# Last down projections by token tiles, norms tile by tile, pooling units in a ring of five banks

## The reference

```python
for l in range(DEPTH):                       # DEPTH = 2
    # mixer: layer 0 conv + sliding window; layer 1 pooling + dilated attention
    xp = xp + mixer(rms_norm(xp, norm_mix[l]))
    xp = xp + cross_attn(rms_norm(xp, norm_ca[l]), mk, mv, w_ca_q[l], w_ca_o[l])
    xp = xp + swiglu(rms_norm(xp, norm_ffn[l]), w_ffn_in[l], w_ffn_out[l])
y = rms_norm(xp, norm_final)

def rms_norm(x, g):
    return x * rsqrt(mean(x * x, axis=-1, keepdims=True) + 1e-6) * g
def swiglu(h, w_in, w_out):                  # hidden width 2816
    g, u = split(h @ w_in, 2, axis=-1)
    return (silu(g) * u) @ w_out
# pooling of layer 1, group g of four, windows 2, 4, 8, 16:
#   uc = (h @ w_in)[group];  d = windowed_mean(uc) - uc;  y = (d @ pool_w[g]) * pool_scale
```

## Time and profile before

| | us |
|---|---|
| median of 3 runs | 3047.67 |
| range of the runs | 3040.66 to 3049.91 |
| profiled execution, its own time | 3039.79 |
| its span in the profile | 3038.0 |
| mean granted clock of TensorE in it | 0.983 of full |

### The profile page before, as it was taken

The page is one execution under the profiler, slowest core; times in us unless marked ns, Lnnn a source line. Parts: engine busy times, 40 slices in busy tenths (PEclk is TensorE's granted clock), DMA queues, the critical chain, the costliest instruction groups (busy, mean ns, idle before and its releaser), DMA issues.

```text
span 3038.0 us, 58274 instructions
## 1 busy us (share of the span) xinstructions
PE 2878.4 (95%) x21187; PEld 2733.0 (90%) x21187; DVE 1646.5 (54%) x3338; ACT 795.4 (26%) x1820; POOL 1319.7 (43%) x1135
## 2 busy tenths in 40 slices
PE   7999999998899999999899998999997999999996
PEld 6888999988899999999787777988897999999996
DVE  5555642258655656556733336522378565565657
ACT  4333322132212221222313335212223211222112
POOL 2222343334556666565221102333335666566561
PEclk9999999999999999999999999999998999999998
DMA  3011133311111111111122211234310111111112
GB/s 128 29 34 35 56 118 126 142 66 42 43 42 55 46 51 55 41 55 49 43 80 77 78 70 57 76 131 140 112 42 28 56 55 41 55 41 55 55 41 70
DMA packets 52534, 198.83 MB, mean 65 GB/s; under 512 B 6960, under 2 KB 14000, under 8 KB 49080
## 3 DMA queue, kind: packets, MB, share of 16 engines
q1 hardware_dynamic: 36912, 130.51, 13.5%
q10 hardware_dynamic: 15504, 66.71, 6.0%
HBM read 184.34 MB, written 13.10 MB: 65 GB/s over the span
## 4 chain that ended last, share of the span: by engine, by line
PE 86%; DVE 7%; issue 3%; ACT 2%; POOL 1%; DMA 0%; ACTq 0%; DVEq 0%; SPq 0%; POOLq 0%
PE linear L696 46%; PE ps_scores L981 12%; PE ps_turned L981 8%; PE ps_mixed L981 4%; PE linear L981 4%; PE ps_mixed L836 2%; PE ps_turned L800 1%; PE ps_turned L1141 1%; PE ps_scores L764 1%; PE ps_mixed L1171 1%; PE ps_scores L1117 1%; DVE g_lo L1803 1%; PE linear L764 1%; PE ps_mixed L832 1%; DVE rs L1773 1%
## 5 line engine op out<-in xcount | busy, mean ns | idle before, releaser
L561 POOL TENSOR_TENSOR w_lo<-w_raw,w_hi 128x512 fp32r<-128x512 f32 x492 | 682.7, 1397 | 257.1 <-ACT w_hi L1251 232.0
L557 POOL TENSOR_SCALAR w_hi<-w_raw 128x512 fp32r<-128x512 f32 x324 | 216.3, 681 | 1210.9 <-PE linear L696 1032.5
L696 PE MATMUL linear<-h_hi,w_hi 128*128 128x344 f32 x1200 | 399.5, 333 | 36.7 <-POOL w_lo L561 13.1
L696 PE MATMUL linear<-h_lo,w_hi 128*128 128x344 f32 x1200 | 387.6, 323 | 0.0
L696 PE MATMUL linear<-h_hi,w_lo 128*128 128x344 f32 x1200 | 387.2, 323 | 0.0
L2195 DVE TENSOR_TENSOR x<-linear,x 128x344 f32<-128x344 f32 x528 | 271.7, 515 | 150.0 <-PE linear L696 147.5
L696 PE MATMUL linear<-hid_hi,w_hi 128*128 128x344 f32 x1056 | 339.6, 322 | 6.9 <-issue 6.8
L696 PE MATMUL linear<-hid_hi,w_lo 128*128 128x344 f32 x1056 | 339.8, 322 | 0.0
L696 PE MATMUL linear<-hid_lo,w_hi 128*128 128x344 f32 x1056 | 339.3, 321 | 0.0
L981 PE MATMUL ps_scores<-c,w_hi 128*128 128x258 f32 x1584 | 307.3, 286 | 21.3 <-DVE c L1990 13.3
L696 PEld LDWEIGHTS linear<-h_hi,w_hi 128*128 128x128 f32 x1200 | 229.1, 191 | 55.5 <-issue 45.9
(11 more groups left out here) (314 smaller groups left out, 6359.6 us busy)
## 6 DMA issues: line engine op xcount, KB each, us to landing
w_raw<-in_w SPq DMA_DIRECT2D x246, 512.0 KB, 3.5
kv_slotc<-in_mem_cache_k ACTq DMA_DIRECT2D x8, 2048.0 KB, 8.1
kv_slotc<-in_mem_cache_v ACTq DMA_DIRECT2D x8, 2048.0 KB, 10.1
kv_slot<-in_dil_k ACTq DMA_DIRECT2D x4, 1536.0 KB, 6.6
kv_slot<-in_dil_v ACTq DMA_DIRECT2D x4, 1536.0 KB, 6.4
out_y<-answer ACTq DMA_DIRECT2D x6, 688.0 KB, 3.4
x<-in_x ACTq DMA_DIRECT2D x2, 1376.0 KB, 10.2
out_dil_v_out<-v ACTq DMA_DIRECT2D x4, 516.0 KB, 3.1
```

The source lines that it names most:

```text
L557: pool.tensor_scalar(out, src, 1.0, 0.0, ALU.mult, ALU.add).then_inc(sem["hi_split"], 1)
L561: return pool.tensor_tensor(out, src, hi.bitcast(F32), ALU.subtract).then_inc(sem[event], 1)
L696: mm = pe.matmul(out, w[:, slot, cols], a, start=(k == 0 and j == 0), stop=(k == n - 1 and j == 2))
```

## The change

- In `ffnend0` and `ffnend1` the down projection runs by tiles: for each tile unit 0's four chunks, then unit 1's. The second weight slot is marked as started only in the last tile. The first tile needs two of the four hidden quarters, not all.
- In layer 0, the sums of squares are no longer 24 adds on DVE but three `tensor_reduce` over the eight squares of a tile. In layer 1, POOL adds them, 21 adds of 128x344; PE multiplies them with one column of `ones`, so that the sum of each token stands on a partition; ACT and DVE take root and reciprocal of 128x2 and 88x1 elements; ACT spreads the result on a diagonal; PE multiplies `ones` with it; and DVE makes `answer` straight from that PSUM bank. The output stores keep their place in ACT's order, behind all of this.
- `pool1` uses banks 0, 1, 2, 6, 7 in turn, without `enter`. `pool_map(0)` stands behind the third unit, `pool_map(3)` behind the v unit. The tables of the pooling part are loaded earlier.
- In the first pair, T2, T3 and T4 of kp 3 are made from B12 and a difference held in `hid_val`; three of the four early low parts of kp 2 are made later; the third to fifth product are read out of their banks ahead of the reciprocals they stood behind; the first two gates are scaled after all three roots. ACT casts the first weight block of the next pair behind the first silu, not behind the fourth.

```diff
     if name == "pool1":
-        return three("dve") * 4
+        return [(b, "dve") for b in (0, 1, 2, 6, 7, 0, 1, 2, 6, 7, 0, 1)]
     if name == "att1pre":
-        return three("dve")
+        return [(b, "dve") for b in (2, 6, 7)]
...
+OTHER_RING = {"pool1": (-2, -1, 0, -2, -2), "att1pre": (-4, -3, -2), "att1_0": (-4, -3, -2)}
...
+                def down_by_tiles(ph, p):
+
+                    for t in range(3):
+                        if t < 2:
+                            pe.wait_ge(sem["hid_lo"], at("hid_lo", ph, 0, 2 + 2 * t))
+                        for u in range(2):
+                            if t == 0:
+                                pe.wait_ge(sem["half_split"], at("half_split", ph, 0, u + 1))
+                            for n in range(4):
+                                chunk(ph, 0, p, u, n, t, n == 0 and t == 2 * u,
+                                      at("unit_split", ph, 0, 2 + u + 1) if t == 0 and n == 0 else None)
+                                p += 1
+                            if l == 1 and t and u == 0:
+                                column_sums(t - 1)
+                                if t == 2:
+                                    spread_inverse(0)
+
+                def column_sums(t):
+
+                    pe.wait_ge(sem["added"], at("added", "into_final", 0, (CH - 1) * (t + 1)))
+                    a, b = TILES[t]
+                    for j, o in enumerate(range(a, b, P)):
+                        m = min(P, b - o)
+                        mm = pe.matmul(sum_banks[t][0:m, 384 + j:385 + j], rs[:, o:o + m], ones[:, 0:1], start=True, stop=True)
+                    mm.then_inc(sem["summed"], 1)
...
+                def spread_inverse(t):
+
+                    pe.wait_ge(sem["diagonal"], at("diagonal", "norm_final", 0, t + 1))
+                    for o in range(0, TILE, P):
+                        m = min(P, TILE - o)
+                        mm = pe.matmul(sum_banks[t][:, o:o + m], ones[0:m, :], diagonal[0:m, t, o:o + m], start=True, stop=True)
+                    mm.then_inc(sem["spread_out"], 1)
...
+                down_by_tiles(f"ffnend{l}", pair(f"ffnend{l}", 0, 0, 0))
+                if l == 1:
+                    column_sums(2)
+                    spread_inverse(1)
+                    spread_inverse(2)
...
+            def behind(g, t):
+
+                if (g, t) in ((0, 1), (1, 0), (1, 1)):
+                    sums(g + t - (g == 0), at("added", "into_mix1", 0, g + t + (g > 0)))
+                if (g, t) == (2, 2):
+                    pe.wait_ge(loads["pool1"], 64)
+                    pool_map(0)
+                if (g, t) in ((3, 0), (3, 2)):
+                    pool_map(1 + t // 2)
...
-                if g:
-                    pool_map(g - 1)
+                         after=lambda t: behind(g, t))
+            unit("att1pre", 0, 0, 0, TILES, h_hi, h_lo, slot=first_slot("att1pre"))
             pool_map(3)
-            enter("att1pre")
-
-            pe.wait_ge(sem["pooled_out"], at("pooled_out", "pool1", 0, 12))
-            unit("att1pre", 0, 0, 0, TILES, h_hi, h_lo, slot=first_slot("att1pre"))
...
+                for n in range(1, CH):
+
+                    pool.wait_ge(sem["squared"], at("squared", "into_final", 0, CH * t + n + 1))
+                    if n > 1:
+                        pool.wait_ge(sem["added"], at("added", "into_final", 0, (CH - 1) * t + n - 1))
+                    pool.sem_inc(gate_sem["pool"], 1)
+                    pool.tensor_tensor(rs[:, a:b], sq_all[:, 0, a:b] if n == 1 else rs[:, a:b], sq_all[:, n, a:b], ALU.add
+                                       ).then_inc(sem["added"], 1)
...
-                gates(f"ffnpre{l}", 0, 0)
-                for b in (0, 1):
-                    cast(b, f"ffnpre{l}", 0, 1, 1, 0)
+                gates(f"ffnpre{l}", 0, 0, 1, {1: lambda: cast(0, f"ffnpre{l}", 0, 1, 1, 0), 3: lambda: cast(1, f"ffnpre{l}", 0, 1, 1)})
...
+
+                for t in range(3):
+                    for n in range(CH):
+                        added(t, n)
+                        past_waits()
+                        square_of(t, n)
+                        if t and n == 5:
+                            root_columns(t - 1)
+                        if t and n == 6:
+                            diagonals(t - 1)
+                root_columns(2)
+                diagonals(2)
...
+                b12, difference = hid_val[:, 0, FIRST], hid_val[:, 1, FIRST]
                 value(2, "B11", "B11")
                 value(3, "B11", "B11")
-                value(3, "T2", "B11")
-                low(2, "B11")
-                low(3, "B11")
                 add(3, 4)
                 dve.wait_ge(sem["freed_dve"], at("freed_dve", source, 3, 5))
-                value(3, "T2", "B12", "above")
+                value(3, None, "B12", b12)
+                low(2, "B11")
+                made(27)
+                count[0] += 1
+                dve.tensor_tensor(difference, b12, combination("val", 3, "B11"), ALU.subtract).then_inc(sem["t_made"], 1)
                 made(28)
-                count[0] += 1
-                dve.tensor_tensor(combination("val", 3, "T2"), combination("val", 3, "T2"), combination("above", 3, "T2"),
-                                  ALU.subtract).then_inc(sem["t_made"], 1)
+                low(3, "B11")
                 dve.wait_ge(sem["tile_done"], at("tile_done", source, 3, 6))
-                made(29)
-                count[0] += 1
-                dve.tensor_scalar(combination("val", 3, "T1"), combination("val", 3, "T2"), -1.0, None, ALU.mult
-                                  ).then_inc(sem["t_made"], 1)
...
+                pre = f"ffnpre{l}"
+                read(pre, 0, 0, 2, None, gate[:, 0, FIRST], None, None)
+                gate_read(pre, 0, 0, 3)
                 inverse_root(0)
+                gate_read(pre, 0, 0, 4, scaled=False)
                 inverse_root(1)
-                dve.wait_ge(sem["rsqrted"], at("rsqrted", ph, 0, 2))
-                gate_read(f"ffnpre{l}", 0, 0, 2)
-                gate_read(f"ffnpre{l}", 0, 0, 3)
                 inverse_root(2)
+                dve.wait_ge(sem["rsqrted"], at("rsqrted", ph, 0, 3))
+                for c, half in QUARTERS[:2]:
+                    dve.tensor_tensor(gate[:, c, half], gate[:, c, half], rs[:, half], ALU.mult).then_inc(sem["gate_ready"], 1)
...
+                    if b == 4:
+                        hid_low(ph, 0, 0)
+                    if b == 5:
+                        hid_low(ph, 0, 2)
+                hid_low(ph, 0, 1)
...
+                    done = 0
+                    for k in range(3 * CH):
+                        add_chunk(k)
+                        if k >= 4 and k % 4 < 3:
+                            low(done)
+                            done += 1
+                    for k in range(done, 2 * CH):
+                        low(k)
+                    total_of_tile(0)
+                    for k in range(2 * CH, 3 * CH):
+                        low(k)
+                    total_of_tile(1)
+                    return
+                for k in range(3 * CH):
+                    add_chunk(k)
+                    if k == 2 * CH - 2:
+                        inverse_columns(0)
+                    if k == 3 * CH - 2:
+                        inverse_columns(1)
+                    if k >= 20:
+                        answer_of(0, k - 20)
+                for c in range(4, CH):
+                    answer_of(0, c)
...
+                dve.tensor_reduce(rs[:, a:b], sq_all[:, :, a:b].rearrange("p c n -> p n c"), AX_X, ALU.add).then_inc(sem["added"], 1)
...
+                    if g == 0 and t == 0:
+                        total_of_tile(2)
+                        dve.wait_ge(sem["added"], at("added", "into_mix1", 0, 3))
+                        chained(dve.memset(pool_u[:, 0:POOL_PAD], 0.0))
```

More of the change, by code:

```diff
@@ L1063, in _ @@
             ffn(0)
-            enter("pool1")
             def pool_map(g):
@@ L2198, in ffn @@
                 order = [(half, t, n) for half in range(2) for t in range(3) for n in range(4)]
-                for b in range(4, 7):
+                for b in (5, 6):
                     gate_read(f"ffnpre{l}", 0, 0, b)
```

283 lines of the change are left out of this document (158 added, 125 removed).

## The result

The changed kernel takes 3013.32 us (median of 4 runs, 3010.11 to 3016.09), the kernel before 3045.94 (median of 4). The ratio is 0.9894, interval 0.9875 to 0.9912: 1.1% faster. The forecast was 2997, range 2984 to 3010. The direction was right, the size was not: the profiled executions differ by 26.5 us in span (3038.0 and 3011.5), where the sum promised 46.5.

A forecast was written before the change was run, and what follows sets the result against it. PE, busy 95%, was taken to bound the kernel, with gains where it waits, mostly for DVE. Terms -28.6, -2.2, -12.4 and -3.3 sum to -46.5, giving 2993.3 from 3039.79, 3001.2 by the median; 2997 was said, range 2984 to 3010.

The forecast's parts named there:

- Pooling stage, the five banks and the maps: Layer 0, down projection's end to v's end: DVE frees banks and means before PE wants them; 64.7 for 93.3, -28.6.
- Pooling stage, the price of the reduction: Layer 0 sums of squares: each reduction of 2752 inputs per partition takes 3.2 us, at 1.18 ns an input.
- slack said to be 2 to 5 us everywhere: Layer 0 pooling stage: DVE has sums, banks and means ready 2 to 5 us early; one us of stalls granted.
- First gate pairs: First gate pair of both layers: DVE's shorter path brings the weight's low part earlier, -6.2 a layer, -12.4 in all.
- four low parts of 0.63: First gate pair, layer 1: DVE's four low parts ahead of the first root priced at 0.63 us each.
- I add 0.8 for contention: First gate pair: 0.8 us allowed for contention, moving the weight's low part from 2321.6 to 2322.4, against 2328.64 before.
- lower bound of 2 a layer: First gate pair: gain of only 2 us a layer if low parts stretch as one of 1.75 did beside POOL.
- Rival A: First gate pair: PE's half-speed products make reads late, keeping 2 to 3 us of 12.4; about 3007, chance 0.14.
- Rival B: Pooling stage: DVE bounds it, POOL stretching its two-input operations; some 9 us come back, 3006, chance 0.12.
- Down projections: Layer 0 down projection: start wait falls from 3.41 to 0.8 us, 2.7 of stalls granted; 26.1 in all, -2.2.
- The end: Layer 1 down projection and output: stores wait in ACT's order, finishing 23.3 us behind PE's last piece; 3034.7 against 3038.0, -3.3.
- Rival E: Pooling stage: strided reduction far dearer, 22 us each removing the whole gain; slower than before, chance 0.02.

The follow-up runs named there:

- experiment 1: Changed kernel with each of the three layer 0 reductions replaced by three additions of halves: 3008.9 us against 3013.3, pooling stage 66.1 us.
- experiment 2: Changed kernel with the third reduction reading neighbouring numbers, not ones 4128 bytes apart (sums then wrong): that reduction 3.02 us in place of 5.28.
- experiment 4: Kernel before, POOL held from weight splits and additions until DVE's last low part: first gate pairs 42.0 and 44.2 us, before 44.9 and 43.1.
- experiment 3: Changed kernel, POOL held until DVE's last low part: splits and additions held, pairs 38.9 and 39.0 us, whole 3010.2; additions alone, 41.3 and 41.4.
- experiment 6: Changed kernel with output stores on SP's queue as answers are made and the third tile's small reciprocal earlier: span ends at 3005.1 us.

## Why the prediction was wrong

- **Pooling stage, the five banks and the maps: right.** No wait for a bank, a window or a mean is left; with the sums in time PE alone fills the stage (66.0 us; 64.7 forecast). The sum's "half of the 0.84 shown for two" misreads its row: those two matmuls are one sum of squares. From start to start the three sums take 1.6 us, so that costs little; the rest of the gap is said in experiment 1.
- **Pooling stage, the price of the reduction: wrong.** The step was "I take the low end, since the row is the same operation, also in a strided order". It measured 1.92 to 2.05 ns an input, not 1.18, 5.3 to 5.6 us a tile. The slack said to be 2 to 5 us everywhere then did not cover two long reductions ahead of the third sum. With the half-speed stretch behind the wait that is 6.7 us (experiments 1 and 2). The bound of 18.3 from the reciprocal was never near, but a value between was there to be taken, and the kernel's own adds of 1.5 ns an element, from SBUF, were the nearer row. The Trainium skill, "VectorE: DVE Perf Modes" (Rules for kernel authors), advised against the reduction; experiment 1 agrees with its advice, experiment 2 shows that for neighbours the operation is no slower than additions.
- **First gate pairs: wrong.** The steps that failed are "four low parts of 0.63" and "I add 0.8 for contention". DVE's operations were counted at the price that they had in layer 1 before, away from POOL's two-input operations. By starting PE's products 3 to 4 us earlier the change let POOL start earlier too, and there the two met; in layer 0, whose timeline the prediction did not read, they had met before (four low parts in 4.00 us, experiment 4) and still do. Held apart, the pair is 3.1 to 3.3 us shorter (experiment 3). Read against 6.2 a layer, the change itself gave 2.9 and 0.8, and 5.9 and 4.1 with POOL held. What layer 1 then lacks is one wait of DVE for the fifth product, 1.16 us, and the factors of the first two roots, 1.27 and 0.98 us beside POOL's held work where the sum had 0.45. The lower bound of 2 a layer named the cause and was still too high for layer 1, which had not paid for it before. (The sum's own terms give 2321.5 and not 2322.4, a slip of 0.9.) The Trainium skill, "SBUF - State Buffer" (Who interferes with whom), says that a DVE operation with two SBUF inputs contends with a POOL operation that reads SBUF; the traces agree (0.63 to 1.71 us). The prediction weighed that rule at the end of the kernel, where nothing came of it, and not here.
- **Rival A had the size, and little of the mechanism.** It kept 2 to 3 us of 12.4; 3.7 were kept. But it blamed PE's products at half speed; with POOL held PE is as slow behind its wait (0.80 for two matmuls) and the gain is there. Half speed does cost something in this pair: the 1.1 us of layer 1 in experiment 4, and perhaps part of the 1.16 above, which was not tried. **Rival B** named POOL stretching DVE's operations, but in the pooling stage, where it cost nothing that experiment 1 did not remove.
- **Down projections: right in kind, in layer 0 half the size in this execution.** The start falls to 0.56 us from 3.41. The stalls are one wait of 1.96 us, and the half-speed stretch behind it, which comes and goes.
- **The end: right.** 23.3 us forecast behind the last piece, 23.2 measured, and the stores did wait for ACT's order (experiment 6). The down projection ahead of it took 28.6 in place of 26.7. POOL's additions took 0.92 each and 0.17 between, 1.09 in place of 0.96, so that PE waited 2.78 us for the last sum.
- **Rival E** did not come: the reduction cost 5.6, not 22.
- **The range was too narrow.** Two terms failed to the same side, and A and B, which have about their sizes, had been taken as exclusive. Both together give 3007 + 9 = 3016, near what came; that is luck in part, since B's 9 us were to come from stretched operations and the 6.7 came from the reductions.

## What to carry to other kernels

Price a strided reduction from a row with its own memory and distance, or add halves: eight squares 4128 bytes apart cost 5.3 us in one reduction and 3.0 in three additions. When the same stage stands in two layers, read both: here layer 0 showed the contention before the change. When a change starts one engine earlier, look up what the engine beside it does in the new interval, and count two-input operations of DVE and POOL that meet at the stretched price. Where several terms share a bias (everything priced quiet), the range must hold them failing together.

## What the runs showed of the hardware

- A TENSOR_REDUCE of 344 outputs from 2752 fp32 inputs in SBUF took 3.02 us with the inputs of a sum next to each other and 5.28 with 4128 bytes between them.
- Two-input fp32 operations of DVE on 516 columns took 0.63 us alone and 1.71 beside two-input operations of POOL, whose 512 columns took 1.27 alone and 1.5 to 1.8 then. Beside a POOL operation with one input it was the other way in layer 1 of the kernel before: DVE's stayed at 0.63 and POOL's went from 0.62 to 3.60. In layer 0 of the same execution that POOL operation took 0.99 beside the first of DVE's four.
- The same wait of 1.96 us was followed by about 4 us at half clock in four of eight executions in layer 0 and in three of the same eight in layer 1, and by none in the others.
